# A decoder trunk on one core: expert columns in two groups of 1536 and 1280, a ring of eight 12 KB slots, and the jobs' rows moved by ScalarE's queue

## The chip, the cores and the metric

The program runs on one core of one Trainium2 chip. The metric is device time in microseconds (us) of one execution. Everything is computed in float32 or in pieces of it.

## The reference

Two layers over 256 tokens of width 1024. Layer 0 is an attention over selected keys and a dense SwiGLU of width 2816; layer 1 is a stick-breaking attention and a mixture of 8 experts of width 2816, of which each token uses two. The part that the change is about:

```python
dense_gates = jnp.sum(jax.nn.one_hot(top_idx, N_EXPERTS, dtype=jnp.float32) * gates[..., None], axis=1)
y = jnp.zeros_like(tok)
for e in range(N_EXPERTS):
    y = y + dense_gates[:, e:e + 1].astype(tok.dtype) * swiglu(tok, w_gate_up[e], w_down[e])
```

where `swiglu(u, w_gate_up, w_down)` is `(silu(u @ gate) * (u @ up)) @ w_down`. The gate and up weights of one expert are 1024 x 5632, the down weights 2816 x 1024: 34.6 million bytes per expert in float32, 276.8 million for the eight.

## The kernel before

**Stages.** The program is written engine by engine, with semaphores. Attention of layer 0 comes first, then the dense SwiGLU in 11 steps of 256 columns, then the attention of layer 1, the router, and the expert stage, which takes the last three fifths of the time. Weights of the early stages come through `up_ring` (4 slots of 16 KB per partition) and `dn_ring` (4 slots of 8 KB), one step ahead of another; SyncE (SP) issues these transfers in program order, each after a wait that its slot is free.

**The expert stage** is a row of jobs. A job is one expert with up to 96 slots of tokens (`SLOTS`), so there are 8 jobs as long as no expert has more than 96 tokens. Each job takes its 96 rows of the normed stream from `x_rows` in DRAM, and leaves 96 rows of result in `y_rows`; at the very end each token gathers its two rows of `y_rows`. Before the stage, GpSimd (POOL) fills both arrays with zeros (`clear`), then scatters the tokens' rows into `x_rows` by an indirect transfer. In each job POOL, in `save`, fetches the next job's rows (`fetch`: four transfers of 32 rows x 3 x 256 columns) and stores this job's (`m_y`, 96 x 1024). Its small `tick` operations only carry waits.

**Tiles of a job.** The gate and up weights of a job are 12 tiles (`E_UP`), in three groups of 1024, 1024 and 768 columns (`E_COLS`): per group two gate tiles and two up tiles, each with 4 of the 8 blocks of 128 rows. They sit in 6 slots of 16 KB: the four of `up_ring`, and `up_more0` and `up_more1`, which lie over `up_hi` and `up_lo`, buffers of the earlier stages. SP loads each tile by two transfers. The down weights are 11 tiles (`STEPS`) of 8 KB per partition, in 6 slots.

TensorE (PE) multiplies with the 96 tokens as weights, 32 at a time, on four column quarters of the array at once (`on_third`): the array's four quarters each take 64 of every 256 columns. The profile shows each of these products as two instructions. After the two gate tiles of a group ScalarE (ACT) applies silu from PSUM into `m_hid`; after the two up tiles VectorE (DVE) multiplies (`hidden_step`) and transposes into `m_hT`, from where PE takes its weights for the down tiles. The semaphores for these three are `e_silu`, `e_raw` and `e_hT`. In step i PE does up tile i, then down tile i - 4, if there is one (`E_DN_LATE = 4`): down tile 0 comes after up tile 4, and the last three down tiles fall into the next job's steps. Steps 0 to 2 of the next job run inside the job before (`FIRST = 3`).

**The order of SP.** For each step SP waits until PE has done the tile whose slot is wanted, issues the two transfers of the tile six ahead, then waits for a down slot and issues a down tile. Queues are in order: what stands behind a wait waits too.

## Time and profile before

| | us |
|---|---|
| median of 3 runs | 1124.64 (1124.53 to 1125.79) |
| the profiled execution | 1125.06 |
| its span in the trace | 1123.2 |

| | share of the span |
|---|---|
| PE busy (matmuls) | 99% |
| DVE busy | 27% |
| ACT busy | 23% |
| POOL busy | 4% |

Starts are in us from the span's start. PE's matmuls are pipelined, so its busy share alone does not say that it is at its peak; how far apart the starts of two tiles lie does. "PEld" is the weight load, which lies beside the matmuls. The granted clock of PE is at full speed in the whole of the expert stage. DMA rates are in GB/s, with 1 GB/s = 1000 bytes per us.

### The profile page before, as it was taken

The page shows a single profiled execution, that of the slowest core. Times are in us where ns is not written, and L with a number is a line of the kernel's source. Part 1 is how long each engine was busy: PE and PEld are TensorE (multiplying, and loading weights), DVE is VectorE, ACT ScalarE, POOL GpSimd, SP SyncE. Part 2 cuts the span into 40 slices and gives each one's busy share as a digit, 9 for nine tenths or more (in the row PEclk, how much of TensorE's full clock was granted, in tenths as well). Part 3 has the DMA queues.
Part 4 walks back from the last instruction along what each step waited for, and adds up shares of the span by engine and source line. Part 5 has one row for each costly group of instructions (what it writes and reads, how often), then busy time and mean ns, then how long its engine had stood idle before and what let it go on. Part 6 is the DMA issues. An engine that isn't in the chain of part 4 may idle for free.

```text
span 1123.2 us, 32541 instructions
## 1 busy us (share of the span) xinstructions
PE 1108.6 (99%) x15020; PEld 865.9 (77%) x15020; DVE 308.0 (27%) x454; ACT 254.6 (23%) x384; POOL 44.5 (4%) x111
## 2 busy tenths in 40 slices
PE   9999999999999999999999999999999999999998
PEld 7768999999899876789987779875576576566565
DVE  4785645545564341010010010010010010010121
ACT  4775534344546631000000001001000000000000
POOL 0000010000000004000000000000100100100100
PEclk9999999999999999999999999999999999999999
DMA  9636789797156279999999999999999999999994
GB/s 336 221 114 225 255 268 332 258 342 267 30 197 226 75 311 377 387 400 411 385 412 411 389 412 410 389 411 411 391 409 412 374 406 411 379 396 413 395 410 167
DMA packets 117301, 371.37 MB, mean 331 GB/s; under 512 B 7272, under 2 KB 34320, under 8 KB 105904
## 3 DMA queue, kind: packets, MB, share of 16 engines
q1 hardware_dynamic: 109776, 343.78, 79.5%
q0 software_dynamic: 7168, 25.43, 6.9%
q8 instruction: 120, 1.97, 0.7%
q10 hardware_dynamic: 224, 0.09, 0.0%
q14 instruction: 13, 0.11, 0.0%
HBM read 347.65 MB, written 21.63 MB: 329 GB/s over the span
## 4 chain that ended last, share of the span: by engine, by line
PE 85%; DMA 6%; SPq 5%; DVE 3%; ACT 2%; issue 1%; ACTq 0%; DVEq 0%
PE pair L936 55%; PE pair L534 8%; PE pair L535 7%; PE pair L536 7%; DMA up_more<-in_moe_w_gate_up 4%; DMA dn_ring<-in_dense_w_down 2%; SPq L433 2%; PE pair L570 1%; SPq L456 1%; SPq L461 1%; PE pair L596 1%; DVE up_lo L1575 1%; ACT up_hi L1067 1%; PE pair L551 0%; PE pair L635 0%
## 5 line engine op out<-in xcount | busy, mean ns | idle before, releaser
L936 PE MATMUL pair<-up_ring,work 128*32 128x256 f32 (+1 forms) x6144 | 357.8, 366 | 1.5 <-DMA up_ring<-in_moe_w_gate_up 0.9
L936 PEld LDWEIGHTS pair<-up_ring,work 128*32 128x32 f32 x6144 | 252.4, 109 | 80.6 <-issue 2.7
L936 PE MATMUL pair<-dn_ring,e_mem 128*32 128x256 f32 (+1 forms) x2016 | 183.9, 450 | 0.0
L936 PE MATMUL pair<-up_more,work 128*32 128x192 f32 (+1 forms) x3072 | 167.6, 353 | 0.8 <-DMA up_more<-in_moe_w_gate_up 0.6
L936 PEld LDWEIGHTS pair<-up_more,work 128*32 128x32 f32 x3072 | 122.4, 109 | 34.5 <-DMA up_more<-in_moe_w_gate_up 2.1
L1969 DVE TENSOR_TENSOR e_mem<-e_mem,pair 128x768 f32<-128x768 f32 (+1 forms) x24 | 21.3, 887 | 438.2 <-PE pair L936 438.2
L936 PEld LDWEIGHTS pair<-dn_ring,e_mem 128*32 128x32 f32 x2016 | 104.1, 109 | 47.9 <-issue 0.2
L534 PE MATMUL pair<-uT_hi,up_hi 128*128 128x256 f32 x480 | 135.6, 282 | 0.8 <-DVE uT_lo L1589 0.6
L535 PE MATMUL pair<-uT_lo,up_hi 128*128 128x256 f32 x480 | 134.8, 281 | 0.0
L536 PE MATMUL pair<-uT_hi,up_lo 128*128 128x256 f32 x480 | 134.8, 281 | 0.0
L1575 DVE TENSOR_TENSOR up_lo<-up_ring,up_hi 128x2048 fp32r<-128x2048 f32 x46 | 105.1, 2290 | 98.1 <-ACT up_hi L1067 98.1
L1382 ACT ACTIVATE e_mem<-pair 128x768 f32<-128x768 f32 (+1 forms) x24 | 18.2, 757 | 474.8 <-PE pair L936 474.8
L1067 ACT ACTIVATE up_hi<-up_ring 128x2048 fp32r<-128x2048 f32 x46 | 87.7, 1912 | 86.6 <-PE pair L536 81.5
L936 PE MATMUL pair<-dn_more,e_mem 128*32 128x256 f32 (+1 forms) x1152 | 105.0, 450 | 0.0
L534 PEld LDWEIGHTS pair<-uT_hi,up_hi 128*128 128x128 f32 x480 | 90.4, 188 | 2.1 <-issue 1.3
L535 PEld LDWEIGHTS pair<-uT_lo,up_hi 128*128 128x128 f32 x480 | 90.5, 188 | 0.4
L536 PEld LDWEIGHTS pair<-uT_hi,up_lo 128*128 128x128 f32 x480 | 90.4, 188 | 0.0
L936 PEld LDWEIGHTS pair<-dn_more,e_mem 128*32 128x32 f32 x1152 | 59.0, 109 | 26.8
L534 PE MATMUL pair<-up_hi,uT_hi 128*128 128x512 f32 x128 | 51.7, 404 | 1.1 <-DVE uT_lo L1599 1.1
L1977 DVE COPY q_T<-pair 96x256 f32<-96x256 f32 x8 | 3.4, 420 | 179.1 <-PE pair L936 179.1
L535 PE MATMUL pair<-up_lo,uT_hi 128*128 128x512 f32 x128 | 50.6, 395 | 0.0
L536 PE MATMUL pair<-up_hi,uT_lo 128*128 128x512 f32 x128 | 50.5, 395 | 0.0
(300 smaller groups left out, 824.7 us busy)
## 6 DMA issues: line engine op xcount, KB each, us to landing
up_ring<-in_moe_w_gate_up SPq DMA_DIRECT2D x96, 1024.0 KB, 14.0
dn_ring<-in_moe_w_down SPq DMA_DIRECT2D x56, 1024.0 KB, 19.6
dn_more<-in_moe_w_down SPq DMA_DIRECT2D x32, 1024.0 KB, 18.0
up_more<-in_moe_w_gate_up SPq DMA_DIRECT2D x32, 1024.0 KB, 14.2
up_ring<-in_moe_w_gate_up SPq DMA_DIRECT2D x32, 768.0 KB, 13.6
up_more<-in_moe_w_gate_up SPq DMA_DIRECT2D x32, 768.0 KB, 14.4
up_ring<-in_dense_w_gate_up SPq DMA_DIRECT2D x22, 1024.0 KB, 8.5
dn_ring<-in_dense_w_down SPq DMA_DIRECT2D x11, 1024.0 KB, 12.9
```

The source lines that it names most:

```text
L433: sp.dma_start(ffn_up(n % RING)[:, :, g, :], dup[:, :, g, FSTEP * i:FSTEP * (i + 1)])\
L456: sp.dma_start(expert_cols(i)[:, 2 * part:2 * part + 2, :], src.rearrange("e p k c -> (e p) k c"))\
L461: sp.dma_start(expert_dn_tile(m), src.rearrange("e p c -> (e p) c")).then_inc(expert_dn_in(m), 16)
L534: pe.matmul(ps, a_hi, b_hi, start=start, stop=False, skip_group_check=shared)
L535: pe.matmul(ps, a_hi, b_lo, start=False, stop=False, skip_group_check=shared)
L536: return pe.matmul(ps, a_lo, b_hi, start=False, stop=stop, skip_group_check=shared)
L570: mm = pe.matmul(bank[2 * t + g][:, 0:I_HALF], uT_in[:, k, P * t:P * t + P], index_tile(half)[:, j, I_HALF * g:I_HALF * g + I_HALF], start ...
L936: return pe.matmul(out, a, w, start=start, stop=stop, tile_position=(0, THIRD * place), skip_group_check=True)
L1067: return act.activation(out_, in_, ACT.Copy, scale=scale)
L1382: act.activation(m_hid[:, 0:3 * cols].rearrange("p (n c) -> p n c", n=3), gate_ps[:, 0:768].rearrange("p (n c) -> p n c", n=3)[:, :, 0:col ...
L1575: dve.tensor_tensor(buffer(up_lo, n, 2048), raw_piece(n), buffer(up_hi, n, 2048).bitcast(f32), ALU.subtract).then_inc(up_l, 1 + unsplit)
L1969: dve.tensor_tensor(v, v, up_ps[:, 0:768].rearrange("p (n c) -> p n c", n=3)[:, :, 0:cols], ALU.mult).then_inc(e_raw, 1)
```

## The change

The gate and up columns of an expert come in two groups, of 1536 and 1280 columns. A tile holds 2 blocks of 128 rows instead of 4, so there are 16 tiles per job, 4 gate and 4 up tiles per group, each loaded by one transfer. They go through one ring of 8 slots of 12 KB, `e_ring`, which lies over `up_ring`, `up_hi` and `up_lo`: the same 96 KB per partition as before. Gate and up results take three PSUM banks each, the down results the two between. The down tiles are done in steps 8, 9, 10, 12, 13, 15, 16, 18, 19, 21 and 22 of a job (`DN_STEP`), and the first 7 steps of the next job run inside the job before. The jobs' rows are fetched and stored by ACT. The zero fill of `y_rows` starts as soon as its source is set, and that of `x_rows` is cut into 11 pieces, one per step of the dense SwiGLU. The core of the diff:

```diff
-E_COLS = (1024, 1024, 768)
+E_COLS = (1536, 1280)
 GROUPS = len(E_COLS)
-E_UP = 4 * GROUPS
+E_UP = 8 * GROUPS
+E_RING = 8
+E_SLOTS = (3, 4, 0, 1, 2, 5, 6, 7)
+X_PARTS = STEPS
...
+        dn_ring = sb("dn_ring", [P, RING, 2048])
+        with nc.sbuf_tensor("e_ring", [P, E_RING, 3072], f32) as e_ring:
+            pass
         up_ring = sb("up_ring", [P, RING, 4096])
-        dn_ring = sb("dn_ring", [P, RING, 2048])
-        with nc.sbuf_tensor("up_more0", [P, 4096], f32) as up_more0:
-            pass
         up_hi = sb("up_hi", [P, 2, 2048], f32r)
-        with nc.sbuf_tensor("up_more1", [P, 4096], f32) as up_more1:
-            pass
         up_lo = sb("up_lo", [P, 2, 2048], f32r)
         with nc.sbuf_tensor("dn_more", [P, 2, 2048], f32) as dn_more:
             pass
...
-        gate_ps, up_ps = pair[0], pair[3]
+        gate_ps, up_ps = e_ps[:, 0:3, :], e_ps[:, 5:8, :]
...
-        FIRST = 3
+        FIRST = 7
         DN_LATE = 2
-        E_DN_LATE = 4
+        DN_STEP = (8, 9, 10, 12, 13, 15, 16, 18, 19, 21, 22)
...
-                g, c0 = i // 4, sum(E_COLS[:i // 4])
-                for part in range(2):
-                    k = 4 * (i % 2) + 2 * part
-                    src = eup[bass.ds(e, 1), :, k:k + 2, i % 4 // 2, c0:c0 + E_COLS[g]]
-                    sp.dma_start(expert_cols(i)[:, 2 * part:2 * part + 2, :], src.rearrange("e p k c -> (e p) k c"))\
-                      .then_inc(expert_in(i), 16)
+                g, k, c0 = i // 8, 2 * (i % 4), sum(E_COLS[:i // 8])
+                src = eup[bass.ds(e, 1), :, k:k + 2, i % 8 // 4, c0:c0 + E_COLS[g]]
+                sp.dma_start(expert_cols(i), src.rearrange("e p k c -> (e p) k c")).then_inc(expert_in(i), 16)
...
             for i in range(RING):
                 sp.wait_ge(up_l, split_end(T_MOE + i - RING))
-                if i == RING - 1:
-                    sp.wait_ge(o_ps, 4)
-                    sp.wait_ge(dn_l, 2 * STEPS)
-                    expert_dn(2, 0)
-                    expert_dn(3, 0)
                 expert_up(i, 0)
-            expert_dn(4, 0)
-            expert_dn(5, 0)
+            expert_up(RING, 0)
+            sp.wait_ge(o_ps, 4)
+            sp.wait_ge(dn_l, 2 * STEPS)
+            for m in range(2, E_DN_RING):
+                expert_dn(m, 0)
             sp.wait_ge(up_used, 2 * T_MOE)
-            for i in range(RING, E_RING):
+            for i in range(RING + 1, E_RING):
                 expert_up(i, 0)
 
             def job(k, e, next_e, first=False, last=False):
-                for i in range(E_RING, E_UP + E_RING):
+                for step in range(E_UP):
+                    i = step + E_RING
                     if i < E_UP or not last:
-                        sp.wait_ge(up_used, tile_done(i - E_RING, k))
+                        sp.wait_ge(up_used, tile_done(step, k))
                         expert_up(i % E_UP, e if i < E_UP else next_e)
-                    m = i - E_DN_LATE
-                    if m < STEPS and not (first and m < E_DN_RING):
-                        sp.wait_ge(dn_used, job_free(m, k))
-                        expert_dn(m, e)
-                    if STEPS <= m < STEPS + 2 and not last:
-                        sp.wait_ge(dn_used, job_free(m - STEPS, k + 1))
-                        expert_dn(m - STEPS, next_e)
+                    for m in range(STEPS):
+                        loaded_at = 7 if m == 5 else DN_STEP[m - 6] if m > 5 else DN_STEP[m + 6] - E_UP
+                        if step == loaded_at and not (first and m < E_DN_RING):
+                            sp.wait_ge(dn_used, job_free(m, k))
+                            expert_dn(m, e)
...
-                g = tile // 4
+                g = tile // 8
                 pe.wait_ge(expert_in(i), job_up_arrived(tile, job))
-                if i < 2:
-                    pe.wait_ge((first_u_act, e_u_now)[i], 1)
-                    pe.wait_ge(first_u_dve, i + 1)
+                if i < 4:
+                    pe.wait_ge(*((first_u_act, 1), (first_u_dve, 1), (e_u_now, 1), (first_u_dve, 2))[i])
                 elif tile == 0:
                     pe.wait_ge(e_u_now, job + 1)
-                if tile % 4 == 0 and i > 0:
+                if tile % 8 == 0 and i > 0:
                     pe.wait_ge(e_silu, group_done(g - 1, job))
-                if tile % 4 == 2 and i > 2:
+                if tile % 8 == 4 and i > 4:
                     pe.wait_ge(e_raw, group_done(g - 1, job))
-                ps, cols = (gate_ps, up_ps)[tile % 4 // 2], hidden_cols(g)
+                ps, cols = (gate_ps, up_ps)[tile % 8 // 4], hidden_cols(g)
                 w = expert_cols(i).rearrange("p k (m c) -> p k m c", c=256)
-                for j in range(4):
-                    k_row = 4 * (tile % 2) + j
+                for j in range(2):
+                    k_row = 2 * (tile % 4) + j
                     for n in range(3):
                         rows = m_u_now[:, SLOTS * k_row + THIRD * n:SLOTS * k_row + THIRD * n + THIRD]
                         for place in range(4):
-                            out = part_of(ps, place)[:, 256 * n:256 * n + cols].rearrange("p (m c) -> p m c", c=64)
+                            out = ps[THIRD * place:THIRD * place + THIRD, n, 0:cols].rearrange("p (m c) -> p m c", c=64)
                             mm = on_third(out, rows, w[:, j, :, 64 * place:64 * place + 64], place,
-                                          k_row == 0 and n != 1, k_row == KD - 1)
+                                          k_row == 0, k_row == KD - 1)
                 mm.then_inc(up_used, 1)
...
-                if i % 4 == 0:
-                    pe.wait_ge(e_hT, group_done(i // 4, k))
+                if i % 6 == 0:
+                    pe.wait_ge(e_hT, group_done(i // 6, k))
...
             def iteration(k, i, last=False):
+                if i == 8 and last:
+                    pe.wait_ge(e_pick, 2)
+                    for t in range(NT):
+                        mm = pe.transpose(bank[4][0:SLOTS, 256 + P * t:256 + P * t + P], m_pick[:, t, :], ident)
+                    mm.then_inc(e_pickT, 1)
                 if i < E_UP or not last:
                     expert_up(k, i)
-                if i == 6 and last:
-                    pe.wait_ge(e_pick, 2)
-                    for t in range(NT):
-                        mm = pe.transpose(bank[5][0:SLOTS, P * t:P * t + P], m_pick[:, t, :], ident)
-                    mm.then_inc(e_pickT, 1)
-                if 0 <= i - E_DN_LATE < STEPS:
-                    expert_dn(k, i - E_DN_LATE)
+                if i == 8 and last:
+                    pe.wait_ge(e_pickT_sb, 1)
+                if i in DN_STEP:
+                    expert_dn(k, DN_STEP.index(i))
...
+            def fetch(j):
+
+                act.wait_ge(x_out, 16 * 2 * NT)
+                act.wait_ge(x_free, j)
+                for place in range(4):
+                    part = slice(THIRD * place, THIRD * place + THIRD)
+                    src = x_rows[bass.ds(j * SLOTS, SLOTS), 256 * place:256 * place + 256]
+                    act.dma_start(m_x[part, :].rearrange("t (n c) -> t n c", n=3),
+                                  src.rearrange("(n t) c -> t n c", n=3)).then_inc(m_x_in, 16)
+
+            def save(k):
+
+                act.wait_ge(e_y_act, k + 2)
+                act.wait_ge(e_y_dve, k + 2)
+                act.dma_start(y_rows[bass.ds(k * SLOTS, SLOTS), :], m_y).then_inc(y_out, 16)
 
             def iteration(k, i, last=False):
+                if i == FIRST and not last:
+                    fetch(k + 1)
+                if i == 8 and last:
...
+                if i == DN_STEP[-1]:
                     result(k)
-                if i == 7 and last:
-                    act.wait_ge(e_pickT, 1)
-                    copy(m_pickT, bank[5][0:SLOTS, 0:TOK]).then_inc(e_pickT_sb, 1)
+                    if not last:
+                        save(k)
...
-            pool.wait_ge(up_used, 2 * (T_DENSE + 3))
 
             def clear(rows, first, end, done):
 
...
                                m_y.unsqueeze(1).to_broadcast([SLOTS, end - first, DM])).then_inc(done, 16)
 
             clear(y_rows, NEXP - 1, JOBS, y_cleared)
-            clear(x_rows, 1, 12, x_cleared)
-            clear(x_rows, 12, JOBS, x_cleared)
+            for part in range(X_PARTS):
+                pool.wait_ge(up_used, 2 * (T_DENSE + part))
+                clear(x_rows, 1 + (JOBS - 1) * part // X_PARTS, 1 + (JOBS - 1) * (part + 1) // X_PARTS, x_cleared)
...
-            pool.wait_ge(x_out, 16 * 2 * NT)
-
-            def save(k):
-
-                pool.wait_ge(y_saved, k + 1)
-                pool.wait_ge(x_free, k + 1)
-                pool.tensor_tensor(tick, tick, tick, ALU.mult).then_inc(tick_done, 1)
-                fetch(k + 1)
-                pool.wait_ge(e_y_act, k + 2)
-                pool.wait_ge(e_y_dve, k + 2)
-                pool.dma_start(y_rows[bass.ds(k * SLOTS, SLOTS), :], m_y).then_inc(y_out, 16)
-                pool.wait_ge(tick_done, k + 1)
-                pool.wait_ge(y_out, 16 * k + 16)
-                pool.tensor_tensor(tick, tick, tick, ALU.mult).then_inc(y_saved, 1)
-
-            with pool.Fori(0, NEXP - 1) as k:
-                save(k)
             last_job = pool.value_load(n_last_job[0:1, 0:1], min_val=NEXP - 1, max_val=JOBS - 1)
-            with pool.If(last_job > NEXP - 1):
-                with pool.Fori(NEXP - 1, JOBS - 1) as k:
-                    save(k)
-            pool.wait_ge(y_saved, last_job + 1)
-            pool.wait_ge(x_free, last_job + 1)
+            pool.wait_ge(y_out, 16 * last_job + 16)
+            pool.wait_ge(e_u, last_job + 1)
...
+                if i == FIRST and last:
                     dve.wait_ge(e_gather, 1)
                     pick(k)
+                if i % 8 == 7 and i < E_UP:
+                    hidden_step(k, i // 8)
+                if i == DN_STEP[-1]:
+                    result(k)
                 if i == 9 and not last:
```

**PE, first job**, around the first down tile: `up_ring`, `up_more` and `e_ring` are the gate and up weights, `dn_more` a down tile, `e_mem` the hidden values. Before:

```order
L936 MATMUL pair<-up_ring,work 32x256 [waits up_in1]
L936 MATMUL pair<-up_ring,work 32x256 x47
L936 MATMUL pair<-up_more,work 32x256 [waits e_silu,e_up_in0]
L936 MATMUL pair<-up_more,work 32x256 x47
L936 MATMUL pair<-dn_more,e_mem 32x512 [waits e_y_act,e_y_dve,e_hT,e_dn_in0]
L936 MATMUL pair<-dn_more,e_mem 32x512 x2
```

And of the change:

```order
L924 MATMUL e_ps<-e_ring,work 32x384 [waits e_up_in7]
L924 MATMUL e_ps<-e_ring,work 32x384 x23
L924 MATMUL e_ps<-e_ring,work 32x320 [waits e_silu,e_up_in3]
L924 MATMUL e_ps<-e_ring,work 32x320 x23
L924 MATMUL pair<-dn_more,e_mem 32x512 [waits e_y_act,e_y_dve,e_hT,e_dn_in0]
L924 MATMUL pair<-dn_more,e_mem 32x512 x2
```

Between the last up tile of a group and the first down tile, which waits for `e_hT`, there stood a tile of 48 products with 256 columns; now there stands one of 24 products with 320.

**SP, start of the expert weights**: the first loads of the stage, some of them while the attention of layer 1 still runs. Before:

```order
L461 DMA dn_more<-in_moe_w_down 128x2048
L456 DMA up_ring<-in_moe_w_gate_up 128x2x1024 [waits up_l]
L456 DMA up_ring<-in_moe_w_gate_up 128x2x1024
L456 DMA up_ring<-in_moe_w_gate_up 128x2x1024 [waits up_l]
L456 DMA up_ring<-in_moe_w_gate_up 128x2x1024
L456 DMA up_ring<-in_moe_w_gate_up 128x2x1024 [waits up_l]
L456 DMA up_ring<-in_moe_w_gate_up 128x2x1024
L461 DMA dn_ring<-in_moe_w_down 128x2048 [waits dn_l,o_ps,up_l]
L461 DMA dn_ring<-in_moe_w_down 128x2048
L456 DMA up_ring<-in_moe_w_gate_up 128x2x1024 x2
L461 DMA dn_ring<-in_moe_w_down 128x2048 x2
```

And of the change:

```order
L452 DMA dn_more<-in_moe_w_down 128x2048
L448 DMA e_ring<-in_moe_w_gate_up 128x2x1536 [waits up_l] x4
L448 DMA e_ring<-in_moe_w_gate_up 128x2x1536
L452 DMA dn_ring<-in_moe_w_down 128x2048 [waits dn_l,o_ps]
L452 DMA dn_ring<-in_moe_w_down 128x2048 x3
L448 DMA e_ring<-in_moe_w_gate_up 128x2x1536 [waits up_used]
L448 DMA e_ring<-in_moe_w_gate_up 128x2x1536 x2
```

The three tiles that go ahead of the fourth wait for `up_l` were 2 x 1024 KB each and are one transfer of 1536 KB each; two tiles instead of one then stand behind the fourth wait.

**ACT, one job in the loop**: `x_rows` and `y_rows` are the jobs' rows in DRAM, `u` and `q_T` the buffers that they go to and come from. These transfers stood on POOL. Of the change:

```order
L1386 ISA [waits x_free]
L1386 DMA u<-x_rows 32x3x256
...
L1370 ACTIVATE e_mem<-e_ps 128x960 [waits e_hT]
...
L1370 ACTIVATE e_mem<-e_ps 128x1152 [waits e_hT]
...
L1055 ACTIVATE q_T<-pair 96x512 [waits y_out]
L1055 ACTIVATE q_T<-pair 32x256 x2
...
L1393 DMA y_rows<-q_T 96x1024
```

The fetch stands ahead of the silu of the second group (960 elements), the store behind the last result copies.

## Rows read from the trace of the kernel before

**Rows 1.** The page: PE's busy time, the 40 slices in GB/s, the instruction queue

```profile
PE 1108.6 (99%) x15020; PEld 865.9 (77%) x15020; DVE 308.0 (27%) x454; ACT 254.6 (23%) x384; POOL 44.5 (4%) x111
...
GB/s 336 221 114 225 255 268 332 258 342 267 30 197 226 75 311 377 387 400 411 385 412 411 389 412 410 389 411 411 391 409 412 374 406 411 379 396 413 395 410 167
...
q8 instruction: 120, 1.97, 0.7%
```

**Rows 2.** Timeline of ACT: start, us, group-0 silu of jobs 1 and 2

```profile
518.26 0.81 ACT L1382 ACTIVATE e_mem<-pair 128x768 f32<-128x768 f32 x1 [14.78 <-PE pair L936]
...
603.79 0.81 ACT L1382 ACTIVATE e_mem<-pair 128x768 f32<-128x768 f32 x1 [14.78 <-PE pair L936]
```

**Rows 3.** Waits of PEld from 424 us: total, times, longest

```profile
PEld pair L936 <- issue: 2.9, 5, 1.3
PEld pair L936 <- DMA up_more<-in_moe_w_gate_up: 2.1, 3, 1.1
PEld pair L936 <- DMA up_ring<-in_moe_w_gate_up: 1.7, 3, 1.4
```

**Rows 4.** Windows of one job each: engines' busy us, PE clock, DMA share, GB/s

```profile
525.50:611.00 85.50, 85.50 (x1553) 76.02 (x1549) 8.27 (x10) 4.67 (x8) 3.13 (x7) 1.00 1.02 402
867.70:953.20 85.50, 85.50 (x1556) 54.38 (x1549) 8.07 (x10) 4.66 (x8) 3.12 (x7) 1.00 1.02 397
```

**Rows 5.** The chain that ended last, its end: start, us, what

```profile
1081.64 18.39 DMA up_more<-in_moe_w_gate_up
...
1100.08 14.47 PE pair L936 x192
```

**Rows 6.** Timeline of PE: a tile and a down tile of job 1, the stall at 235

```profile
235.34 0.47 PE L534 MATMUL pair<-dn_hi,hid_hi 128*128 128x512 f32 x1 [1.35 <-DVE hid_lo L1805]
...
533.00 0.40 PE L936 MATMUL pair<-up_more,work 128*32 128x256 f32 x2
...
538.18 0.61 PE L936 MATMUL pair<-dn_more,e_mem 128*32 128x512 f32 x2
...
540.76 0.40 PE L936 MATMUL pair<-up_more,work 128*32 128x256 f32 x2
```

**Rows 7.** Timeline of DVE: the multiply after the up tiles at 533

```profile
533.72 0.95 DVE L1969 TENSOR_TENSOR e_mem<-e_mem,pair 128x768 f32<-128x768 f32 x1 [4.32 <-PE pair L936]
```

**Rows 8.** Groups of DVE by form from 430 us: count, busy us, mean ns

```profile
L1971 DVE STREAM_TRANSPOSE e_mem<-e_mem 128x768 f32<-128x768 f32 x16 | 16.3, 1019 | 0.6
L1969 DVE TENSOR_TENSOR e_mem<-e_mem,pair 128x768 f32<-128x768 f32 x16 | 15.3, 954 | 263.5 <-PE pair L936 263.5
...
L1971 DVE STREAM_TRANSPOSE e_mem<-e_mem 128x576 f32<-128x576 f32 x8 | 6.3, 789 | 0.3
...
L1969 DVE TENSOR_TENSOR e_mem<-e_mem,pair 128x576 f32<-128x576 f32 x8 | 6.0, 754 | 174.7 <-PE pair L936 174.7
```

**Rows 9.** Short windows, columns as in the windows of a job

```profile
390.00:400.00 10.00, 10.00 (x47) 8.16 (x46) 3.93 (x4) 3.65 (x4) 0.00 (x0) 1.00 0.09 11
538.00:552.00 14.00, 14.00 (x243) 13.37 (x239) 0.00 (x0) 0.81 (x1) 2.41 (x5) 1.00 1.03 357
552.00:577.00 25.00, 25.00 (x471) 23.14 (x466) 3.88 (x4) 0.65 (x1) 0.00 (x0) 1.00 1.02 411
585.00:607.00 22.00, 22.00 (x396) 17.02 (x391) 1.57 (x2) 1.66 (x2) 0.00 (x0) 1.00 1.02 411
```

**Rows 10.** Timeline of SP's queue: start, us, what it issued

```profile
351.58 47.32 SPq L456 DMA_DIRECT2D up_ring<-in_moe_w_gate_up  x6
403.62 0.82 SPq L461 DMA_DIRECT2D dn_ring<-in_moe_w_down  x2
...
944.51 8.45 SPq L456 DMA_DIRECT2D up_ring<-in_moe_w_gate_up  x2
```

**Rows 11.** Timeline of POOL: the clears of x_rows, one job's fetch

```profile
151.24 1.83 POOL L1435 DMA_DIRECT2D x_rows<-q_T  x2
...
538.76 2.37 POOL L1467 DMA_DIRECT2D u<-x_rows  x4 [0.47 <-issue]
```

More of the change, by code:

```diff
@@ L263, in program @@
         e_pick, e_pickT, e_pickT_sb = sem("e_pick"), sem("e_pickT"), sem("e_pickT_sb")
-        e_up_in = [sem(f"e_up_in{n}") for n in range(2)]
+        e_up_in = [sem(f"e_up_in{n}") for n in range(E_RING)]
         e_dn_in = [sem(f"e_dn_in{n}") for n in range(2)]
@@ L337, in job_up_arrived @@
         def job_up_arrived(i, k):
-            s = expert_slot(i)
-            ahead = up_arrived(max(n for n in range(T_MOE) if n % RING == (T_MOE + s) % RING)) if s < RING else 0
-            uses = [expert_slot(j) for j in range(E_UP)]
-            return k * (32 * uses.count(s)) + (ahead + 32 * uses[:i + 1].count(s))
+            return k * (16 * E_UP // E_RING) + 16 * (i // E_RING + 1)
         def job_dn_arrived(m, k):
@@ L1393, in iteration @@
                 if i == E_UP and not last:
                     gathered(k + 1)
[L1395 to L1397 removed]
+                if i % 8 == 3 and (i < E_UP or not last):
+                    silu_step(k + i // E_UP, i % E_UP // 8)
+                if i == DN_STEP[-1]:
                     result(k)
[L1399 to L1401 removed]
+                    if not last:
+                        save(k)
@@ L1459, in folded @@
                 return v[:, :, 0:1]
-            pool.memset(tick, 0.0).then_inc(y_saved, 1)
-            def fetch(j):
-                for place in range(4):
-                    part = slice(THIRD * place, THIRD * place + THIRD)
-                    src = x_rows[bass.ds(j * SLOTS, SLOTS), 256 * place:256 * place + 256]
-                    pool.dma_start(m_x[part, :].rearrange("t (n c) -> t n c", n=3),
-                                   src.rearrange("(n t) c -> t n c", n=3)).then_inc(m_x_in, 16)
+            pool.memset(tick, 0.0).then_inc(y_out, 16)
             pool.wait_ge(jobs_known, 1)
```

95 lines of the change are left out of this document (42 added, 53 removed).

## The prediction

> **What bounds the kernel now.** I read the page first [rows 1]: PE is busy for 99% of the span, and over the last 25 of the 40 slices the DMA engines move about 400 GB/s. Both could be the bound, so the question is which wait ends last in the expert stage. The timeline of ACT gives the period of a job: the silu of the first group starts at 518.26 and at 603.79, 85.53 us apart [rows 2]. Within that period PE stands still for nothing: PE's waits for the products of the whole stage sum to 2.9 us of "issue" and 2.1 + 1.7 = 3.8 us for tiles of gate and up weights [rows 3]. So for seven jobs PE's own stream sets the pace. The supply does not quite keep up: a job needs 34.6 million bytes of weights and 0.8 million of rows (two times 96 x 1024 x 4), which is 35.4 / 85.53 = 414 GB/s, and the windows of one job each show 402 and later 397, at a full DMA share [rows 4]. The lead of six tiles makes up for it until the last job, where the chain goes through the landing of the last up tile at 1081.64 + 18.39 = 1100.03 us, and 14.5 us of PE behind it [rows 5]. The kernel thus has two bounds within 4 us of each other: PE alone would end 3.8 us earlier, the supply ends it where it ends. An edit that helps one alone gives 3.8 us at most, and an edit that harms one is paid at once or after 3.8 us.
>
> **What the change does to PE.** The streamed columns stay the same: 8 blocks x (1536 + 1280) x 2 against 8 x 2816 x 2. Their rate should too, since a quarter of the array streams one product after another: a tile of 1024 columns and 4 blocks takes 538.18 - 533.00 = 5.18 us, the down tile behind it 2.58, 7.76 together [rows 6]. There are 11 down tiles between up tiles before and after. I take no gain or loss here.
>
> The edit that costs is the place of the first down tile. It waits for `e_hT`, so for DVE's multiply and transpose of the whole first group, and the cover is the one tile in between. From the trace: the multiply starts 533.72 - 533.00 = 0.72 us after the next tile [rows 6, 7]; it takes 0.954 us for 768 elements and 0.754 for 576, the transpose 1.019 and 0.789 [rows 8]. The slopes give 1.35 and 1.48 us for 1152. Longer products end later by 5.18 us / 96 instructions x 4 quarters x 128/256 = 0.11. The hidden values are there 0.72 + 0.11 + 1.35 + 1.48 = 3.66 us after the start of the covering tile. That tile was 5.18 us long; it is now 2 x 1280 of 4 x 1024 columns, 3.24 us. `e_hT` feeds PE's weights, so a weight load and a refill of the quarters come on top: at least 0.05 us (landing 1100.03, PE 1100.08 [rows 5]), at most 0.5; I take 0.25. The stall is 3.91 - 3.24 = 0.67 us per job (0.47 to 0.92), 5.4 us over eight. What is queued behind it on PE is everything. The second group has the next job's first tile and a down tile as cover, but in the last job only the down tile of 2.58 us: 0.72 + 0.05 + 1.15 + 1.25 + 0.25 = 3.42, a stall of 0.8.
>
> Gains on PE: the 3.8 us of DMA waits, if the supply allows it; and of the 2.9 us of "issue", five pauses in the first tiles of the stage [rows 3], where PE eats two instructions per product faster than they come. The gate and up products go from 9216 recorded instructions to 6144, so a tile's worth of columns needs a third fewer. I take 2.0 off (0 to 2.9).
>
> **What it does to the supply.** The bytes per job stay, the ring's 96 KB and the down slots too. But the first three tiles, which go out before the rest while DMA is idle (window 390 to 400: 11 GB/s [rows 9]; six transfers from 351.58, the next at 403.62 [rows 10]), shrink from 2 MB to 1.5 MB each. 1.57 million bytes move behind 403.62, into a stretch that is full to the end: 1.57 million / 411 GB/s = +3.8 us on the supply. Instructions on queue 8 are 1.97 million bytes for 15020 matmuls and as many weight loads, some 65 each [rows 1]; 3072 fewer of each kind take 0.4 million off, -1.0 us.
>
> The rest is relief of unknown size. First, the fetch: in the 14 us around POOL's four transfers at 538.76 [rows 11] the rate is 357 instead of 411 [rows 9], a loss of 54 x 14 = 0.76 million bytes or 1.8 us a job, 12.9 us over seven. It could stay whole (the same 32 x 3 x 256 pieces on the same engines) or go in part. Second, from 700 us on SP itself is held up (two transfers took 8.45 us to issue at 944.51 [rows 10]) and the rate sinks to 397 [rows 4]: 5/402 x 85.5 = 1.1 us a job in three jobs, 3.2 us. With rows of 6 and 5 KB instead of 4 and 3, the same number of pieces in a queue holds more bytes. I take 2.4 us from the second and nothing from the first; the ends are 0 and 16. SP's order behind a held transfer is as before, one tile then one down tile.
>
> The page "DMA: Bandwidth & Descriptors" of the Trainium skill, section "Issuing engines are not separate DMA queues", says that transfers from any engine end on the same 16 DMA engines and that another issuer only saves issue time; by it the dip of 1.8 us a job stays, which is what I chose from the rows. Its section "Why small descriptors are slow (HBM only)" gives some 3 cycles per piece beside one per 32 bytes. An estimate by that page makes the new pieces 0.6% cheaper, about -3.8 us on the supply, and would leave the end where PE's side has it; the trace does not show such a step: with 1024 columns (552 to 577) and with 768 (585 to 607) the rate is 411 both times [rows 9].
>
> **The clears.** In the dense stage POOL clears the rows of 17 + 23 jobs, 15.7 million bytes, in three transfers, the last two at 151.24 [rows 11]; behind them a down tile comes late, and PE stands still 1.35 us at 235.34 [rows 6]. With the y fill early and x in 11 pieces of 0.8 million bytes per step of 17 us I take this stall as gone, -1.4 us (0 to -1.4) on both sides, since all that follows moves up. ACT's new transfers cost it a few us per job; it is busy for 4.7 us of 85.5 [rows 4], and its next silu is four tiles away. If that cover were gone, the silu of the second group would be late, and PE's next job with it.
>
> **The sum**, against the profiled execution's span of 1123.2: PE side -3.8 - 2.0 + 5.4 + 0.8 - 1.4 = -1.0; supply side +3.8 - 1.0 - 1.4 - 2.4 = -1.0. The last tile lands 15.3 us of down weights ahead of the end of the supply instead of 10.2, but 18.6 us of PE follow instead of 14.5; 1.0 us more room for the supply, which I leave as reserve. The end is the later of the two, 1122.2. The profiled execution took 1125.06 and the median is 1124.64, so I subtract from the median: 1123.6.
>
> **The rivals.** A measurement here tells from no change what is over 0.2%, 2.2 us.
> A, the forecast (0.40): both bounds move by -1, own range 1121.4 to 1126.
> B, faster (0.27): the stall at the first down tile is small, at most 0.2 us a job, because PE's quarters are still draining then; the pauses all vanish, and the supply gains from ring and fetch. -3.8 - 2.9 + 1.6 + 0.3 - 1.4 = -6.2, 1118.4. It needs 7.6 us of relief on the supply; for it speak the dips [rows 9], against it the chain of 3.66 us.
> C, slower (0.25): the supply binds. ACT stores and fetches back to back, where POOL waited some 7 us for the store; if the dip grows by 0.4 us a job and the queue gives nothing back, +3.8 - 1.0 - 1.4 + 2.8 = +4.2, 1128.8. It decides from 0.12 us a job on. For it speaks that every DMA second is taken already; against it that the store alone shows no dip (the dip begins at the fetch).
> D, waits only change their name (0.08): the pauses at the start stay, the new stalls take the place of the DMA waits: -3.8 + 5.4 + 0.8 - 1.4 = +1.0, 1125.6.
>
> **The numbers.** Likeliest 1123.6. Range 1118.4 to 1128.8 holds A, D and most of B and C. Faster by over 0.2%: most of B and the low end of A, 0.37. Within 0.2%: 0.39. Slower: most of C and a little of A, 0.24.
>
> **What the new profile would show.** PE waiting for DVE's transpose once a job, 0.5 to 0.9 us, and a period near 86.2 us; no "issue" pauses after 424; no PE stall near 235; windows of a job at 400 GB/s or more in the late jobs; waits for `e_ring` under 2 us. Wrong would make it: a period still at 85.5 (then B), or waits for `e_ring` over 6 us in the last two jobs (then C).

## The result, and the profile after

The changed kernel takes 1117.38 us (median of 4 runs, 1116.90 to 1117.78) against 1124.59 us: ratio 0.9932, 95% interval 0.9920 to 0.9944, so 7.2 us less. The forecast was 1123.6 us with 0.37 on faster. The time lies 1.0 us below the range, beside rival B (1118.4 us, chance 0.27). The prediction was wrong.

The profiled execution has a span of 1115.6 us (before: 1123.2). First the page: PE's busy time, the 40 slices, the instruction queue, and the engines' shares of the chain that ended last, to be laid beside [rows 1].

```profile
PE 1104.4 (99%) x11948; PEld 845.4 (76%) x11948; DVE 306.3 (27%) x438; ACT 253.5 (23%) x376; POOL 27.8 (2%) x71
...
GB/s 338 217 124 308 319 342 310 240 217 212 29 198 218 57 277 416 401 417 417 399 416 416 398 417 416 398 416 416 397 418 416 398 416 416 402 412 416 415 352 93
...
q8 instruction: 96, 1.57, 0.6%
...
PE 95%; DVE 2%; ACT 1%; DMA 0%; issue 0%; ACTq 0%; DVEq 0%
```

The plateau of the DMA engines (the slices of the expert stage without a dip) is 416 to 418 GB/s where it was 409 to 413, and no transfer of expert weights is left in the chain. The windows of one job, early and late (against [rows 4]):

```profile
525.50:610.80 85.30, 85.30 (x1171) 63.76 (x1167) 7.85 (x8) 4.49 (x7) 0.00 (x0) 1.00 1.02 410
867.70:953.00 85.30, 85.30 (x1172) 66.03 (x1165) 7.91 (x8) 4.49 (x7) 0.00 (x0) 1.00 1.02 410
```

A late job is no slower than an early one any more. PEld's waits from 423 us on (against [rows 3]):

```profile
PEld e_ps L924 <- issue: 18.7, 97, 0.2
PEld pair L924 <- issue: 2.5, 8, 0.6
```

There is no wait for a tile at all; 96 of the 97 pauses of 0.2 us lie inside the first eight tiles, one after every fourth weight load, and PE itself has no gap there: its 432 instructions up to the first down tile, from 423.23 to 457.44, are one row. The period, from ACT's timeline (against [rows 2]):

```profile
516.56 1.13 ACT L1370 ACTIVATE e_mem<-e_ps 128x1152 f32<-128x1152 f32 x1 [22.49 <-PE e_ps L924]
...
601.85 1.13 ACT L1370 ACTIVATE e_mem<-e_ps 128x1152 f32<-128x1152 f32 x1 [22.49 <-PE e_ps L924]
```

It is 85.29 us, 0.24 less than before, not 0.7 more. And around the first down tile of job 1 (DVE, then PE; against [rows 6, 7]):

```profile
539.73 1.35 DVE L1948 TENSOR_TENSOR e_mem<-e_mem,e_ps 128x1152 f32<-128x1152 f32 x1 [2.92 <-PE e_ps L924]
541.12 1.38 DVE L1950 STREAM_TRANSPOSE e_mem<-e_mem 128x1152 f32<-128x1152 f32 x1
```

```profile
535.52 7.39 PE L924 MATMUL e_ps<-e_ring,work 128*32 128x384 f32 x96
542.62 2.88 PE L924 MATMUL pair<-dn_more,e_mem 128*32 128x512 f32 x36
```

The row of 96 products is two tiles, the last of 1536 columns and the covering one of 1280. With 3.87 us for the first, the second starts at 539.39; DVE begins 0.34 us later and is done at 542.50, and the down tile starts at 542.62, as early as the tile ahead of it allows. The stall that I had put at 5.4 us is not there. The margin is thin, though: in job 4 one transpose took 1.73 us instead of 1.38, and that period is 85.52 us, 0.23 longer than the others.

Where the 7.6 us between the two spans lie, by five moments: PE's first expert product, DVE's first multiply of job 0 and of job 7, ACT's last copy, and the end. Before they are at 424.71, 448.19, 1046.90, 1113.81 and 1123.2, after at 423.23, 454.47, 1051.70, 1105.90 and 1115.6. From each stretch of a first or last job I subtract PE's bare products: four tiles of 5.12 us, or eight of 3.84, up to the first multiply, and what is left of 84.48 us a job behind it.
- Start of the stage: 1.5 us earlier.
- First group of job 0: 3.0 us over its products before, 0.5 now; 2.5 gained.
- Seven periods: 598.71 against 597.23; 1.5 gained.
- Last job: 66.91 - 64.00 = 2.9 over before, 54.20 - 53.76 = 0.4 now; 2.5 gained.
- After the last product: 0.3 lost.

### The profile page after: what moved, and what is told of

The parts are those of the page before. It is cut to its first block, busy times and chain, and to the rows that moved or that the text cites. A ratio compares the mean times of both kernels' runs of the same rounds, so it can differ in the third digit from the quotient of the medians.

```text
span 1115.6 us, 26142 instructions
## 1 busy us (share of the span) xinstructions
PE 1104.4 (99%) x11948; PEld 845.4 (76%) x11948; DVE 306.3 (27%) x438; ACT 253.5 (23%) x376; POOL 27.8 (2%) x71
## 3 DMA queue, kind: packets, MB, share of 16 engines
q8 instruction: 96, 1.57, 0.6%
## 4 chain that ended last, share of the span: by engine, by line
PE 95%; DVE 2%; ACT 1%; DMA 0%; issue 0%; ACTq 0%; DVEq 0%
PE e_ps L924 41%; PE pair L924 20%; PE pair L522 9%; PE pair L523 9%; PE pair L524 9%; PE pair L558 1%; PE pair L584 1%; DMA norm_rows<-in_b_norm_w 0%; DVE up_lo L1554 0%; PE pair L623 0%; DVE dn_ring L1659 0%; PE pair L917 0%; ACT up_hi L1055 0%; PE pair L860 0%; PE pair L812 0%
## 5 line engine op out<-in xcount | busy, mean ns | idle before, releaser
L924 PE MATMUL e_ps<-e_ring,work 128*32 128x384 f32 (+1 forms) x6144 | 482.3, 459 | 0.0
L924 PEld LDWEIGHTS e_ps<-e_ring,work 128*32 128x32 f32 x6144 | 317.9, 110 | 131.3 <-issue 18.7
L924 PE MATMUL pair<-dn_ring,e_mem 128*32 128x256 f32 (+1 forms) x2016 | 162.9, 450 | 0.0
L924 PEld LDWEIGHTS pair<-dn_ring,e_mem 128*32 128x32 f32 x2016 | 107.0, 110 | 45.2
L1370 ACT ACTIVATE e_mem<-e_ps 128x1152 f32<-128x1152 f32 (+1 forms) x16 | 16.8, 1050 | 361.3 <-PE e_ps L924 361.3
L924 PE MATMUL pair<-dn_more,e_mem 128*32 128x256 f32 (+1 forms) x1152 | 92.4, 450 | 0.0
L1948 DVE TENSOR_TENSOR e_mem<-e_mem,e_ps 128x1152 f32<-128x1152 f32 (+1 forms) x16 | 20.1, 1254 | 228.5 <-PE e_ps L924 228.5
L1055 ACT ACTIVATE q_T<-pair 32x256 f32<-32x256 f32 (+2 forms) x30 | 14.3, 480 | 162.2 <-PE pair L924 153.7
L1055 ACT ACTIVATE work<-q_T 128x768 f32<-128x768 f32 x7 | 5.9, 843 | 119.3 <-PE e_ps L924 119.3
## 6 DMA issues: line engine op xcount, KB each, us to landing
e_ring<-in_moe_w_gate_up SPq DMA_DIRECT2D x64, 1536.0 KB, 20.8
up_ring<-in_dense_w_gate_up SPq DMA_DIRECT2D x22, 1024.0 KB, 10.3
```

The costliest lines, as they stand in the source:

```text
L924: return pe.matmul(out, a, w, start=start, stop=stop, tile_position=(0, THIRD * place), skip_group_check=True)
L1055: return act.activation(out_, in_, ACT.Copy, scale=scale)
L1370: act.activation(m_hid[:, 0:3 * cols].rearrange("p (n c) -> p n c", n=3), gate_ps[:, :, 0:cols], ACT.Silu).then_inc(e_silu, 1)
L1948: dve.tensor_tensor(v, v, up_ps[:, :, 0:cols], ALU.mult).then_inc(e_raw, 1)
```

## The experiments

Some edits are of the changed kernel (1117.38 us), some of the kernel before; each expectation says which. Each was timed beside runs of the kernel before (medians 1124.1 to 1125.1), and the ratio is to these: 0.9932 for the changed kernel itself.

**1. The cover of the first down tile.** PE takes the first down tile ahead of tile 8:

```
+                if i == 8:
...
+                    expert_dn(k, 0)
                 if i < E_UP or not last:
                     expert_up(k, i)
...
-                if i in DN_STEP:
+                if i in DN_STEP[1:]:
```

> The changed kernel with the first down tile of a job ahead of the tile that covers it (tile 8), so that PE stands still for the whole chain of DVE's multiply and transpose: it measures that chain. Theory from the trace of after (0.34 us to the multiply, 1.35 and 1.38): a stall of 3.1 to 3.4 us a job, time 1117.4 + 25 to 27 = 1142.4 to 1144.6. The forecast's chain of 3.91 us: a stall of 3.9 us a job, time 1148.7.

Measured: 1147.42 us, ratio 1.0204 [1.0186, 1.0221], 30 us more. In job 1 (DVE, then PE):

```profile
542.72 1.35 DVE L1950 TENSOR_TENSOR e_mem<-e_mem,e_ps 128x1152 f32<-128x1152 f32 x1 [2.92 <-PE e_ps L924]
544.11 1.38 DVE L1952 STREAM_TRANSPOSE e_mem<-e_mem 128x1152 f32<-128x1152 f32 x1
```

```profile
545.59 2.80 PE L924 MATMUL pair<-dn_more,e_mem 128*32 128x512 f32 x36 [2.91 <-issue]
```

The multiply starts at 542.72, the transpose ends at 545.49, and the down tile starts at 545.59: DVE's chain is 2.77 us and PE follows 0.10 behind it. With the 0.34 before it, 3.2 us, against a cover of 3.24. Of the six periods between the silus of jobs 1 to 7 three are 3.1 us longer, as the first theory has it; the others are 6.1, 4.8 and 4.5 longer, and with them the sum comes to 30. The time alone would have misled: it is above the 1142.4 to 1144.6 expected from the shorter chain and nearer to the 1148.7 of the forecast's, and only the trace tells the chain from what came after it. Windows of the worst (columns as in [rows 4]; the third number from the right is PE's granted clock):

```profile
628.00:631.00 3.00, 3.00 (x40) 1.94 (x31) 0.20 (x1) 0.20 (x1) 0.00 (x0) 1.00 1.03 416
631.00:633.00 2.00, 0.08 (x1) 0.00 (x0) 1.84 (x2) 0.00 (x0) 0.00 (x0) 1.00 0.99 358
633.00:640.00 7.00, 6.01 (x44) 2.95 (x48) 0.89 (x1) 0.00 (x0) 0.00 (x0) 0.51 1.04 371
640.00:643.00 3.00, 3.00 (x48) 1.47 (x44) 0.00 (x0) 0.00 (x0) 0.00 (x0) 1.00 0.47 183
```

PE stood for 2.91 us, and then ran at 1.2 GHz instead of 2.4 until 640. The same stall cost 6.0 us there (from the first group's silu to the second's 49.99 us, against 43.94 in the changed kernel) and 3.1 in job 1, where the clock stayed at 1.00.

**2. Width of the products.** Each gate and up product in two:

```
-                            mm = on_third(out, rows, w[:, j, :, 64 * place:64 * place + 64], place,
+                            for m0, m1 in ((0, 3), (3, cols // 64)):
...
+                                mm = on_third(out, rows, w[:, j, m0:m1, 64 * place:64 * place + 64], place,
...
```

> The changed kernel with each gate and up product cut in two (192 + 192 columns, 192 + 128 in the second group), 12288 products instead of 6144; tiles, ring, transfers and waits stay. Theory W, the width of a product pays for the start pauses and the shorter period: pauses named issue of 2 us or more return in the first job, the period goes from 85.29 back to 85.5 us or more, time 1121 to 1123. Rival S, both came from the supply of weights and from the smaller tiles: no pauses, period 85.3, time 1117 to 1118.

Measured: 1178.03 us, ratio 1.0490 [1.0467, 1.0513]. The direction is theory W's, the size is 60 us and not 4 to 6. PEld's timeline of job 1 shows why (rows that wait; the number of loads is behind the x):

```profile
576.10 2.92 PEld L924 LDWEIGHTS e_ps<-e_ring,work 128*32 128x32 f32 x86 [0.73 <-issue]
...
582.30 3.24 PEld L924 LDWEIGHTS e_ps<-e_ring,work 128*32 128x32 f32 x95 [0.59 <-issue]
...
588.51 0.11 PEld L924 LDWEIGHTS pair<-dn_ring,e_mem 128*32 128x32 f32 x2 [0.63 <-issue]
...
594.71 2.31 PEld L924 LDWEIGHTS e_ps<-e_ring,work 128*32 128x32 f32 x66 [1.51 <-issue]
```

The pauses come every 6.2 us, and between two of them lie 128 products with their 128 loads (at 440.13, 446.34 and 452.27 the row is x128 each time). The instruction queue moved 2.36 MB in 144 packets, 16 KB each, which is 128 products and loads of 64 bytes. So by these distances one packet of instructions takes about 6.2 us to be renewed while the DMA engines are full (their busy share is 1.00 in the window of job 1). The kernel before uses one in 128 x 5.12 / 96 = 6.8 us, a margin of 0.6; the changed kernel in 128 x 7.74 / 96 = 10.3. The page "Runtime: NRT & Kernel Launch" of the Trainium skill, section "Instruction fetch mechanics", has the 16 KiB blocks of 256 instructions, and the trace agrees (16.4 KB a packet). It also says that fetching is hidden; here it is not: PE's weight loads waited 52 us for nothing else that the profile shows.

**3. Size and number of the pieces.** Three ways of fetching a tile by two transfers: both kinds of tile in column halves (3 and 2.5 KB pieces), both by block (6 and 5 KB), or the gate tiles by columns and the up tiles by block. The first of them:

```
+                for half in range(2):
+                    w0, w1 = E_COLS[g] // 2 * half, E_COLS[g] // 2 * (half + 1)
+                    src = eup[bass.ds(e, 1), :, k:k + 2, i % 8 // 4, c0 + w0:c0 + w1]
+                    sp.dma_start(expert_cols(i)[:, :, w0:w1], ...).then_inc(expert_in(i), 16)
```

> The changed kernel with each tile fetched by two transfers of half its columns, so pieces of 3 and 2.5 KB in place of 6 and 5 KB (two issues per tile). Theory P, the size of the pieces is what lifts the rate and with it the last job: the plateau falls from 417 to 411 GB/s or less, PE waits for e_ring in the last jobs, time 1119.5 or more. Theory N, the rate depends on the pieces but the lead is enough without it: plateau 411 or less, no or hardly any waits, time within 1 us of 1117.4. If the plateau stays at 417, the pieces were not its cause.

> The changed kernel with each tile fetched by two transfers of one block each: pieces stay 6 and 5 KB, only the number of transfers doubles. It separates the count of transfers from the size of the pieces. Both theories: plateau 417 GB/s, time within 1 us of 1117.4; if it is slower and the plateau lower, it is SP's issuing, not the pieces, that limits the rate.

> The changed kernel with only the gate tiles cut into two transfers of half the columns (the up tiles in two of one block each, pieces whole): 6144 pieces a job for gate and up weights, the number that the kernel before has (8192 with both cut, 4096 in the change). Theory P, every piece costs time: plateau 411 GB/s as before, about 404 per job, and since PE now asks 415 GB/s, waits for tiles in the last job of 1 to 4 us, time 1118.5 to 1121.5. Rival, only pieces of 2.5 KB are slow: plateau 415 or more, time 1117.4.

Measured: column halves 1129.15 us, ratio 1.0035 [1.0021, 1.0048]; blocks 1117.23 us, 0.9928 [0.9914, 0.9941]; gate tiles alone 1122.70 us, 0.9977 [0.9967, 0.9988]. All DMA packets from 515 to 601 us, in the order before, after, gate tiles, column halves:

```profile
DMA packets 8183, 34.63 MB, mean 403 GB/s; under 512 B 629, under 2 KB 629, under 8 KB 6764
```

```profile
DMA packets 6467, 35.31 MB, mean 411 GB/s; under 512 B 506, under 2 KB 890, under 8 KB 5072
```

```profile
DMA packets 8580, 34.77 MB, mean 404 GB/s; under 512 B 752, under 2 KB 1136, under 8 KB 7202
```

```profile
DMA packets 10472, 34.41 MB, mean 400 GB/s; under 512 B 744, under 2 KB 1128, under 8 KB 9085
```

The rate goes with the number of packets, not with that of transfers: with blocks, twice the transfers, the window 552 to 577 shows 415 GB/s, where the changed kernel has 417 and column halves have 408. From after to column halves 4005 packets more, 250 per engine, make 34.6 MB take 86.5 instead of 84.2 us: 9 ns for each packet of an engine. The same working gives 11 ns for the gate-tile kernel. It doesn't cover all of the old kernel's rate, 403 GB/s with fewer packets than the gate-tile kernel has at 404; what the rest is, these runs don't show. With the number of pieces of the kernel before, the changed kernel has lost 5.3 of its 7.2 us (5.1 by ratio), a little more than expected. PEld's waits in the gate-tile kernel show where (this execution is the slowest of its eight, 1124.69 us):

```profile
PEld pair L929 <- DMA dn_ring<-in_moe_w_down: 4.7, 2, 2.7
PEld e_ps L929 <- DMA e_ring<-in_moe_w_gate_up: 2.0, 4, 1.3
```

With column halves these waits reach 14.2 us (6.9, 3.7 and 3.6), down tiles first.

**4. Release of the ring.** SP waits for both tiles of a pair in the changed kernel; and in the kernel before, PE reports and SP fetches halves of a tile:

```
-                        sp.wait_ge(up_used, tile_done(step, k))
+                        sp.wait_ge(up_used, tile_done(step // 2 * 2 + 1, k))
```
```
-                mm.then_inc(up_used, 1)
+                    if j % 2 == 1:
+                        mm.then_inc(up_used, 1)
```

> The changed kernel with SP waiting for the second tile of a pair before it fetches either again: a step of 3 MB per 7.7 us in place of 1.5 MB per 3.9 us; pieces and slots stay. Theory R, the finer release keeps the DMA engines fed where the ring is full (before they fell to 195 GB/s at 430 to 432): dips below 380 GB/s near 430 to 440 come back, and PE waits for e_ring in the last job, time 1118.5 to 1121. Rival: the lead hides it, time 1117.4 within 1 us.

> The kernel before, with PE reporting each half of a tile (two of its four blocks) and SP fetching each half as it comes free; groups, pieces, clears and rows as before. Theory R: the rate at 430 to 440 rises from 319 to about 400 GB/s, PE's waits for tiles in the last job go from 2.9 us to under 1, time 1124.1 - 2 to 3 = 1121 to 1122. Rival: the last job's waits come from the rate of the whole stage (402 GB/s, dips at the fetch), time 1123.5 to 1124.5.

Measured: 1117.77 us, ratio 0.9933 [0.9920, 0.9947], nothing lost although the window 430 to 440 fell to 365 GB/s; and 1123.80 us, 0.9987 [0.9978, 0.9996], with 406 GB/s there and no pause of PE. The waits of the last job, which theory R had go, grew instead: from DVE's first multiply to ACT's last copy it takes 67.59 us where it took 66.91, so 3.6 us of waits instead of 2.9. Only half of the theory holds: the start was repaired, and 1.3 us came out at the end.

**5. The clears.** The old ones in the changed kernel, the new ones in the kernel before, and the new ones with the fine release:

```
+            pool.wait_ge(up_used, 2 * (T_DENSE + 3))
             clear(y_rows, NEXP - 1, JOBS, y_cleared)
-            for part in range(X_PARTS): ...
+            clear(x_rows, 1, 12, x_cleared)
+            clear(x_rows, 12, JOBS, x_cleared)
```

> The changed kernel with the clears as before: POOL waits for the third dense tile and then clears y and x rows in three transfers. Theory: PE stands still 1.35 us near 235 again and the first expert product moves from 423.2 to about 424.7, time 1118.9. Rival: the stall at 235 belonged to something else, or is made up later, time 1117.4.

> The kernel before with the clears of the change alone: y at once, x rows in eleven pieces, one per dense step. If the supply sets the end of the kernel before and moves with the dense stage: PE's stall at 235 goes, everything moves up, time 1124.6 - 1.4 = 1123.2. Rival: the end of the supply stays where it is (its prefetch starts by other events) and the 1.4 us come back as waits for tiles in the last job, time 1124.6 within 0.5.

> The kernel before with the fine release and the early clears together; products, groups and pieces of 4 and 3 KB stay. The two give 1.3 us (measured) and 1.4 us: 1121.9 if they add up. What is then left to the changed kernel at 1117.4, some 4.5 us, belongs to larger pieces and wider products: waits for tiles in the last job 2.9 us and a period 0.24 us longer in seven jobs.

Measured: 1119.25 us, ratio 0.9951 [0.9937, 0.9964], 1.9 us lost, and the first silu of job 1 is 1.5 us later; 1123.67 us, 0.9992 [0.9983, 1.0001], no difference that can be told; 1121.66 us, 0.9968 [0.9959, 0.9978], about what was added up (3.2 per thousand, against 1.3 and 0.8 measured one by one, each uncertain by 0.9). In the second, PE's first expert product is 1.2 us earlier and the pauses of job 0 are missing as well, so its first group is 3.7 us ahead (444.49 against 448.19). The last job's groups are then 31.8 and 27.2 us apart, where PE alone needs 28.5 and 26.0: 4.5 us of waits instead of 2.9. A part comes back; how much of the clears' 1.2 us stays, these runs don't tell.

**6. Which bound ends the kernel before.** One fetch of the four for a job's rows (three quarters of the rows of jobs 1 to 7 are left out), and the kernel before unchanged:

```
-                for place in range(4):
+                for place in range(1):
...
```

> The kernel before with one of the four transfers that fetch a job's rows (three quarters of the rows of jobs 1 to 7 are left out): it frees the supply of some 0.3 MB and most of the dip a job, and leaves PE's work whole. If the supply alone causes PE's waits in the last job, they vanish and nothing else changes: 1124.6 - 2.9 = 1121.7. Rival: the waits belong to SP's loop end (its gap at 1036 to 1043) and stay, time 1124 or more.

> The kernel before, unchanged, profiled once more: are the pauses of PE in the first job (2.5 us from 437 to 441) and the 2.9 us of waits in the last job there in every execution? If the supply sets the end, an execution without the pauses has more waits in the last job, their sum near 5.4 us, and the same span, 1122.5 to 1124.

Measured: 1120.24 us, ratio 0.9963 [0.9950, 0.9977], PE's waits for tiles all gone, and in its profiled execution the pauses of the first job too; and one execution of 1125.62 us. In the latter the first job has no pause, and PE's timeline of the last job has this row:

```profile
1047.88 7.07 PE L936 MATMUL pair<-up_more,work 128*32 128x256 f32 x96 [2.84 <-DMA up_more<-in_moe_w_gate_up]
```

Its first two groups there are 1078.82 - 1045.08 = 33.74 us apart instead of 28.49, so 5.25 us of waits, as expected (2.5 of pauses and 2.9 of waits before), and the span is 1123.9. In these two executions of the old kernel PE won or lost 2.5 us in the first job and ended within 0.7 us of the same time. With the supply relieved and PE's work whole, the kernel ended 4.8 us earlier (4.2 by ratio). Both say that the supply sets the end.

**7. The rows on POOL.** The changed kernel with the old fetch and store (the diff is that of the change, backwards).

> The changed kernel with the jobs' rows fetched and stored by POOL as before. Theory: the supply has slack now, so the dip at the fetch (357 GB/s over 14 us against about 375 now) costs nothing, no wait for e_ring, time 1117.4 within 1 us. Rival: the transfers on ACT are what keeps the supply ahead; waits for e_ring in the last two jobs, time 1119.5 or more.

Measured: 1117.49 us, ratio 0.9935 [0.9922, 0.9949]. A job runs at 409 to 410 GB/s instead of 410 to 411, and nothing waits. Who issues these transfers is worth nothing here.

**8. Down tiles in pairs.**

```
-        DN_STEP = (8, 9, 10, 12, 13, 15, 16, 18, 19, 21, 22)
+        DN_STEP = (8, 8, 10, 10, 13, 13, 16, 16, 19, 19, 22)
```

> The changed kernel with the down tiles in pairs between gate and up tiles (steps 8, 8, 10, 10, 13, 13, 16, 16, 19, 19, 22): 6 switches a job between the two kinds of tile in place of 11. In the trace a gate or up tile with a down tile takes 0.05 to 0.08 us more than its products. Theory: each switch costs 0.05 us, 5 x 0.05 x 8 = 2.0 us less, time 1115.4. Rival: the cost is per tile, not per switch, or the down tiles come late in pairs, time 1117.4 or more.

Measured: 1130.30 us, ratio 1.0051 [1.0037, 1.0065]. The theory fell. Two tiles of 1280 columns and two down tiles take 11.62 us (630.43 to 642.05), twice the 5.81 of a pair of one and one: the small surplus is not per switch. What made it slower is cover: without the down tile of step 15, PE waits for ACT's copy of the next job's rows:

```profile
668.88 0.84 ACT L1056 ACTIVATE work<-q_T 128x768 f32<-128x768 f32 x1 [17.05 <-PE e_ps L924]
```

```profile
662.06 6.78 PE L924 MATMUL e_ps<-e_ring,work 128*32 128x320 f32 x96
669.82 4.08 PE L924 MATMUL e_ps<-e_ring,work 128*32 128x384 f32 x48 [0.98 <-issue]
```

The copy ends at 669.72 and PE goes on at 669.82. That is 0.98 us in each period, and in the last job nothing is left in front of the second group's transpose, a pause of 3.1 us of the weight loads. Together they are 10 of the 13 us lost; I haven't followed the rest.

## Why the prediction was wrong, point by point

- **The two bounds.** Right, and shown: the supply ends the old kernel, PE alone would have ended it 4 to 5 us earlier (1120.24 us with supply to spare). I had put the lead of PE's side at 3.8 us, PEld's waits; PE's own groups show 2.9 and, with the pauses, 5.4.
- **"The stall is 3.91 - 3.24 = 0.67 us per job ... 5.4 us over eight."** This step failed, and it is the largest. The chain measures 3.2 us. 0.38 of the error is the start: I counted 0.72 us from 533.00 [rows 6], but that row is the first quarter of the array reaching the next tile. The others came until 533.39, and DVE's multiply 0.33 after that. The transpose took 1.38 instead of 1.48, PE followed in 0.10 instead of 0.25, and the 0.11 for longer products did not appear. So of the 6.2 us of stalls in the sum some 0.4 is there: 0.2 in the one period with a slow transpose, and the last job's, +0.8 in the sum, is 0.2 as well: the transpose ends at 1093.35 and the sixth group's down tile starts at 1093.49, where 1090.71 + 2.58 = 1093.29 was possible.
- **"1.57 million bytes move behind 403.62, into a stretch that is full to the end: +3.8 us on the supply."** The stretch was not full. Windows of the old kernel, then one of the changed kernel (columns as in [rows 4]):

```profile
430.00:432.00 2.00, 2.00 (x44) 1.22 (x40) 0.00 (x0) 0.00 (x0) 1.46 (x7) 1.00 0.69 195
430.00:440.00 10.00, 9.70 (x161) 4.95 (x153) 0.00 (x0) 0.89 (x2) 7.32 (x20) 1.00 0.93 319
```

```profile
430.00:440.00 10.00, 10.00 (x128) 4.03 (x124) 0.00 (x0) 1.01 (x1) 7.25 (x21) 1.00 1.02 414
```

From 430 to 440 the old kernel's DMA engines made 319 GB/s: SP had waited for PE's first tile, and the next 2 MB went out only at 430.16. I had read windows before 400 and behind 538 and none between. Smaller tiles come free sooner, and the lost lead is made up there: from 340 to 430 us the changed kernel moved 19.9 million bytes against 20.8, but to 440 it moved 24.1 against 23.9.
- **"I take 2.4 us from the second and nothing from the first."** The supply's relief was mis-sized, and the wrong row was read for it. A job's 35.4 million bytes take 87.6 us at the 404 GB/s of an old job and 86.2 at 410.5, so about 11 us over eight jobs, inside my bounds of 0 and 16; and the fall to 395 to 399 in the late jobs, which both kernels with column-cut tiles show too, is gone with it. I had found no effect of the pieces because 1024 and 768 columns both gave 411 [rows 9]. That reading was wrong twice. PE was on the 768-column tiles from 564 to 588, so partly in both windows; and what counts is what is in flight: SP issued the 768-column tiles at 526 to 548, so in both windows it was mostly pieces of 4 KB. From 526 to 539, with the 3 KB pieces, the rate is 411 as well, but at 9 ns a packet the contrast would be under 2 GB/s (247 packets per million bytes from 528 to 540, 229 from 585 to 607), too little to see in so short a window. The rule that I weighed and set aside pointed the right way: the Trainium skill's page "DMA: Bandwidth & Descriptors", section "Why small descriptors are slow (HBM only)", charges a fixed cost per packet. With its 3 cycles I had estimated 3.8 us for the stage; the runs show about 11 us. The other rule, section "Issuing engines are not separate DMA queues" of the same page of the Trainium skill, held: the dip at the fetch stayed, 374 GB/s in 540 to 552 where it was 351.
- **The pauses, -2.0.** They vanished, 2.5 us in these two traces. But the old kernel has them in one execution and not in the other, and its end doesn't depend on them. That they come from late instruction packets is likely, not shown: the packets were at 427, 430 and then 443 us in the trace with pauses, and every 6 to 8 us in that of the finer release. In the second execution of the old kernel they were at 427, 431 and 441, and PE had no pause. What made one late in one execution stays open.
- **The dense stall, -1.4.** Right on PE's side: 1.5 in the trace, 1.9 by medians. On the supply's side it is at most partly there: in the old kernel the same edit gave 0.8 per thousand, with one per thousand of uncertainty.
- **PE's stream, "no gain or loss".** It gained 0.21 to 0.24 us a period, 1.5 us. With products of 192 columns a tile of 1536 columns and a down tile take 6.48 us, with those of 384 they take 6.46; 0.02 over eleven such pairs is 0.2 a job and could be it. It is argued, not shown.
- **ACT's transfers at nothing.** Right, measured at 0.1 us (0.3 by ratio), both within the noise.

Why the sum came out so low: rival B had the sizes (stall at most 0.2, pauses gone, over 7.6 us of relief) and its 1118.4 us was 1.0 off. Its reasons were only half right. It expected the relief from ring and fetch, but the fetch's dip stayed, a finer release gave the old kernel 1.3 us and a coarser one cost the changed kernel nothing, and most of it came from the size of the pieces; that its number came so near is in part luck. The shares by experiment: supply to spare in the old kernel 4.2 to 4.8 us, clears 1.5 to 1.9, PE's period 1.5; together 7.2 to 8.2, against 7.2 measured.

## What to carry to other kernels

When a stream of transfers is the bound, compare rates by what is in flight (issues and packets of that window), not by what the engines are working on, and count packets: here each cost some 9 to 11 ns of its DMA engine, and a third fewer of them for the streamed tiles was worth 5 us. Before adding a wait, measure its chain from the last part of the array that finishes, not from the first row of the next tile, and look which small copies live under the same cover (a paired order lost 13 us by uncovering two). And a bound that sits just behind another swallows gains: in two executions of the old kernel PE differed by the 2.5 us of the early pauses, and the waits of the last job made up for it.

## What the hardware did that I had not expected

- Instructions are a supply too. With the DMA engines full, 16 KB of them (128 products and loads) took about 6.2 us, going by the pauses; a stream of 192-column products needed them faster and lost 60 us.
- A standstill of PE of 2.9 us was followed by up to 7 us at 1.2 GHz in three jobs of eight, which raised its price from 3.1 to between 4.5 and 6.1 us. At the same length, in the other five it was not.
- Just after the stage began, at 430 to 432 us, the old kernel's rate was 195 GB/s in a stage that its supply bounds: the ring was full, and one release of 2 MB came too late to keep the engines fed.
